# A hybrid decoder trunk: x load and exchanged rows issued later, two norms by Ln/Exp without reciprocals, and new filler counts

## The reference

```python
h = rms_norm(x, norm_g[l]);  p = h @ w_in[l]
z, p_rw, p_ml, p_mla, p_da = split(p)        # 2048 | 1600 | 2056 | 704 | 1536 columns
y = concat(beta0 * rwkv7(p_rw), beta1 * mlstm(p_ml), beta2 * mla(p_mla), beta3 * diff_attn(p_da)) * silu(z)
x = x + y @ w_out[l]
```

```python
# RWKV-7: the keys that are removed from the state are normalised per head of 64
kk = kk / maximum(sqrt(sum(kk * kk)), 1e-12)
# mLSTM, per head of 128: a normaliser, then an RMS norm over the head
h = num / maximum(abs(den), exp(-m))
h = h * rsqrt(mean(h * h) + eps) * g
```

## Time and profile before

| what | value |
|---|---|
| median of 3 runs (lowest, highest) | 2413.65 us (2412.28, 2413.82) |
| the profiled execution's own time | 2416.05 us |
| its span, first to last instruction | 2414.3 us |
| busy: PE, weight loads, DVE, ACT, POOL | 2324.0, 1751.9, 1192.2, 634.9, 1737.8 us |
| mean granted clock of PE | 0.990 |
| moved by DMA | 285.09 MB, mean 118 GB/s |

### The profile page before, as it was taken

One profiled execution on the slowest core, in us unless ns is written; L12 is line 12 of the kernel. 1 busy time (PEld: TensorE's weight loads), 2 busy tenths in 40 slices (PEclk: granted clock), 3 DMA queues, 4 the chain that ended last, 5 costly groups with the idle time before them and its releaser, 6 DMA issues. The chain is left out here.

```text
span 2414.3 us, 38594 instructions
## 1 busy us (share of the span) xinstructions
PE 2324.0 (96%) x16160; PEld 1751.9 (73%) x16160; DVE 1192.2 (49%) x1515; ACT 634.9 (26%) x1133; POOL 1737.8 (72%) x1228
## 2 busy tenths in 40 slices
PE   7999999999999999899999999999999999989999
PEld 6767777777777777677777677777776777767777
DVE  5123346647464773565250323557375546735552
ACT  5222222212221222333341323222222212214421
POOL 3677688768577787687637666878586687877785
PEclk9999999999999999999999999999999999999999
DMA  4623253223234346432445233533242243473323
GB/s 156 187 80 104 83 161 110 84 81 114 84 89 132 118 131 233 151 92 71 148 112 160 79 114 92 154 93 102 66 121 82 81 150 108 131 275 110 86 77 125
DMA packets 164335, 285.09 MB, mean 118 GB/s; under 512 B 28664, under 2 KB 36216, under 8 KB 162624
## 3 DMA queue, kind: packets, MB, share of 16 engines
q1 hardware_dynamic: 108352, 180.93, 27.0%
q10 hardware_dynamic: 55808, 101.69, 12.4%
HBM read 230.89 MB, written 51.64 MB: 117 GB/s over the span
## 5 line engine op out<-in xcount | busy, mean ns | idle before, releaser
L733 POOL TENSOR_SCALAR w_hi<-raw 128x512 fp32r<-128x512 f32 x552 | 905.4, 1640 | 476.3 <-PE ps_proj L774 401.6
L743 POOL TENSOR_TENSOR w_lo<-raw,w_hi 128x512 fp32r<-128x512 f32 (+1 forms) x640 | 836.8, 1308 | 152.6 <-ACT w_hi L1237 97.1
L774 PE MATMUL ps_proj<-h_hi,w_hi 128*128 128x512 f32 (+1 forms) x1760 | 740.1, 421 | 2.0 <-POOL w_lo L743 0.9
L774 PE MATMUL ps_proj<-h_lo,w_hi 128*128 128x512 f32 (+1 forms) x1760 | 691.8, 393 | 0.0
L774 PE MATMUL ps_proj<-h_hi,w_lo 128*128 128x512 f32 x1728 | 678.5, 393 | 0.0
L774 PEld LDWEIGHTS ps_proj<-h_hi,w_hi 128*128 128x128 f32 (+1 forms) x1760 | 331.3, 188 | 113.1 <-issue 29.7
L774 PEld LDWEIGHTS ps_proj<-h_lo,w_hi 128*128 128x128 f32 (+1 forms) x1760 | 331.3, 188 | 75.0
L774 PEld LDWEIGHTS ps_proj<-h_hi,w_lo 128*128 128x128 f32 x1728 | 327.8, 190 | 68.6 <-issue 11.4
L789 PE MATMUL ps_proj<-w_hi,h_hi 128*128 128x512 f32 x448 | 181.1, 404 | 0.4 <-POOL w_lo L743 0.4
L789 PE MATMUL ps_proj<-w_hi,h_lo 128*128 128x512 f32 x448 | 174.9, 390 | 0.0
L789 PE MATMUL ps_proj<-w_lo,h_hi 128*128 128x512 f32 x448 | 174.5, 390 | 0.0
(11 more groups left out here) (349 smaller groups left out, 3132.5 us busy)
## 6 DMA issues: line engine op xcount, KB each, us to landing
raw<-in_w_in_dram SPq DMA_DIRECT2D x480, 256.0 KB, 2.7
raw<-in_w_out_dram SPq DMA_DIRECT2D x128, 256.0 KB, 3.0
projected<-stage ACTq DMA_DIRECT2D x116, 256.0 KB, 2.8
arena<-projected ACTq DMA_DIRECT2D x90, 256.0 KB, 3.1
out_dram<-arena ACTq DMA_DIRECT2D x7, 1024.0 KB, 4.8
gated_hi<-arena ACTq DMA_DIRECT2D x24, 256.0 KB, 2.6
gated_lo<-arena ACTq DMA_DIRECT2D x24, 256.0 KB, 3.2
h_hi<-gated_hi SPq DMA_DIRECT2D x8, 768.0 KB, 13.7
```

Of the source, the lines that this page charges most:

```text
L733: nc.gpsimd.tensor_scalar(hi, src, 1.0, None, ALU.mult).then_inc(s_hi_split, 1)
L743: nc.gpsimd.tensor_tensor(lo, src, hi.bitcast(F32), ALU.subtract).then_inc(s_raw_split, 1)
L774: last = mm(ps_proj[rows, m, :], lhsT, rhs, start=(k == 0 and j == 0), stop=(k == KT - 1 and j == len(products) - 1))
```

## The change

On ACT, the load of x moves from ahead of DA's head 0 to behind head 0's exponentials, and the exchanged rows of the next head move from between the two halves to behind both. kk's norm becomes exp(-0.5 Ln(sum)) on ACT, ahead of the decay's exponentials, and one DVE operation. mLSTM's norm is computed without dividing: PE does the denominator first, ACT squares the numerator, DVE forms eps * d^2 and adds it to the mean, ACT takes Ln and Exp. A tiny Ln (load_ln) is put ahead of three waits, so that ACT's table is loaded there. FILL has new counts.

```diff
-    rw_first=8, rw_lora=(10, 10, 10, 9), rw_factors=(31, 33, 33, 33), ...
+    rw_first=8, rw_lora=(10, 11, 11, 11), rw_factors=(26, 28, 28, 28), ...
-    rw_carried=(2, 2, 2, 2), rw_mean=(3, 3, 3, 3), rw_gate=(13, 14, 13, 12),
-    ml_first=25, ml_qk=(19, 10, 10, 10), ml_s=(8, 7, 7, 6), ml_h=(14, 14, 13, 11), ml_gate=(7, 12, 12, 12),
-    da_first=21, ..., da_half=(12, 17, 15, 16), ...
+    rw_carried=(2, 2, 2, 2), rw_mean=(4, 4, 4, 4), rw_gate=(13, 14, 13, 12),
+    ml_first=25, ml_qk=(19, 13, 13, 13), ml_s=(8, 8, 8, 8), ml_h=(3, 3, 3, 3), ml_gate=(15, 15, 15, 12),
+    da_first=21, ..., da_half=(14, 17, 15, 16), ...
@@ PE, mLSTM
                         for i in range(NT):
-                            mm(ps[:, 0, i * P:T], ml_v[:, i, h * P:(h + 1) * P], ml_s[:, i, i * P:T], ...)
-                        for i in range(NT):
                             last = mm(ps[:, 1, i * P:T], ones, ml_s[:, i, i * P:T], ...)
+                        last.then_inc(s_ml_den_mm, 1)
+                        for i in range(NT):
+                            last = mm(ps[:, 0, i * P:T], ml_v[:, i, h * P:(h + 1) * P], ml_s[:, i, i * P:T], ...)
                         last.then_inc(s_ml_num_mm, 1)
@@ ACT
+                    def load_ln():
+                        link(nc.scalar.activation(table_set, eps_col, ACT.Ln))
@@ ACT, RWKV
                         fill("rw_lora", hp)
+                        load_ln()
+                        act.wait_ge(s_rw_kk_sum, hp + 1)
+                        link(nc.scalar.activation(rw_nr, ps[:, 3, :], ACT.Ln))
+                        nc.scalar.activation(rw_nr, rw_nr, ACT.Exp, scale=-0.5).then_inc(s_rw_kk_root, 1)
                         act.wait_ge(s_rw_decay, hp + 1)
...
                         nc.scalar.activation(rw_wi, rw_c, ACT.Exp, scale=-1.0).then_inc(s_rw_decay_exp, 1)
-                        act.wait_ge(s_rw_kk_sum, hp + 1)
-                        nc.scalar.activation(rw_nr, ps[:, 3, :], ACT.Sqrt).then_inc(s_rw_kk_root, 1)
                         fill("rw_factors", hp)
...
                         fill("rw_mean", hp)
+                        load_ln()
                         act.wait_ge(s_rw_var, hp + 1)
@@ ACT, mLSTM
+                        act.wait_ge(s_ml_num_mm, h + 1)
+                        nc.scalar.activation(ml_sq, ps[:, 0, :], ACT.Square).then_inc(s_ml_h_sq, 1)
                         fill("ml_h", h)
-                        act.wait_ge(s_ml_h_sum, h + 1)
-                        rstd(ml_rs, ps[:, 2, :], P, EPS).then_inc(s_ml_h_rs, 1)
+                        load_ln()
+                        act.wait_ge(s_ml_h_var, h + 1)
+                        link(nc.scalar.activation(ml_rs, ml_den, ACT.Ln))
+                        nc.scalar.activation(ml_rs, ml_rs, ACT.Exp, scale=-0.5).then_inc(s_ml_h_rs, 1)
                         fill("ml_gate", h)
@@ ACT, DA
                     act.dma_start(da_const, ...)
-                    act.dma_start(x_tok, x_dram if tail else a["x"][0]...).then_inc(s_x_prefetched, 16)
                     fill("to_z_da")
...
                             act.wait_ge(s_da_row_max, 2 * h + half + 1)
-                            if half and h < HEADS - 1:
-                                load_da_swapped(h + 1)
                             for b in range(4):
                                 ...   # the exponentials
+                        if h < HEADS - 1:
+                            load_da_swapped(h + 1)
                         if h == 0:
+                            act.dma_start(x_tok, x_dram if tail else a["x"][0]...).then_inc(s_x_prefetched, 16)
                             fill("da_half", h)
@@ DVE, RWKV
-                        link(v.tensor_scalar(rw_nr, rw_nr, 1e-12, None, MAX))
-                        link(v.reciprocal(rw_nr, rw_nr))
-                        link(v.tensor_tensor(rw_kk, rw_kk, rw_nr, MUL))
+                        link(v.scalar_tensor_tensor(out=rw_kk, in0=rw_nr, scalar=1e12, in1=rw_kk, op0=MIN, op1=MUL))
@@ DVE, mLSTM
-                        dve.wait_ge(s_ml_num_mm, h + 1)
+                        dve.wait_ge(s_ml_den_mm, h + 1)
                         link(v.scalar_tensor_tensor(out=ml_den, in0=ps[:, 1, :], scalar=-1.0, in1=ml_nf, op0=MUL, op1=MAX))
-                        link(v.tensor_tensor(ml_den, ps[:, 1, :], ml_den, MAX))
-                        link(v.reciprocal(ml_den, ml_den))
-                        link(v.tensor_tensor(ml_h, ps[:, 0, :], ml_den, MUL))
-                        v.tensor_tensor(ml_sq, ml_h, ml_h, MUL).then_inc(s_ml_h_sq, 1)
+                        link(v.scalar_tensor_tensor(out=ml_den, in0=ps[:, 1, :], scalar=DEN_MIN, in1=ml_den, op0=MAX, op1=MAX))
+                        link(v.scalar_tensor_tensor(out=ml_den, in0=ml_den, scalar=EPS, in1=ml_den, op0=MUL, op1=MUL))
+                        dve.wait_ge(s_ml_h_sum, h + 1)
+                        v.scalar_tensor_tensor(out=ml_den, in0=ps[:, 2, :], scalar=1.0 / P, in1=ml_den, op0=MUL, op1=ADD).then_inc(s_ml_h_var, 1)
                         dve.wait_ge(s_ml_o_tanh, h + 1)
                         dve.wait_ge(s_ml_h_rs, h + 1)
-                        link(v.scalar_tensor_tensor(out=ml_h, in0=ml_h, ..., in1=ml_rs, op0=MUL, op1=MUL))
+                        link(v.scalar_tensor_tensor(out=ml_h, in0=ps[:, 0, :], ..., in1=ml_rs, op0=MUL, op1=MUL))
```

More of the change, by code:

```diff
@@ L39 @@
 MASKED = -1e30
+DEN_MIN = 1e-15
 Z0 = 0
@@ L98 @@
     la_probs=(13, 13, 13, 13), la_turned=(3, 3, 3, 3), la_gate=(4, 4, 4, 4),
-    rw_first=8, rw_lora=(10, 10, 10, 9), rw_factors=(31, 33, 33, 33), rw_turned=(3, 3, 3, 3), rw_v=(2, 2, 2, 2),
+    rw_first=8, rw_lora=(10, 11, 11, 11), rw_factors=(26, 28, 28, 28), rw_turned=(3, 3, 3, 3), rw_v=(2, 2, 2, 2),
     rw_gram=(4, 4, 4, 4), rw_x=(2, 2, 2, 2), rw_level=(1, 1, 1, 1), rw_step=(1, 1, 1, 1), rw_levels=(1, 1, 1, 1),
     rw_pu=(2, 2, 2, 2), rw_local=(4, 4, 4, 4), rw_outer=(1, 1, 1, 1), rw_state=(1, 1, 1, 1), rw_state_last=(0, 0, 0, 0),
-    rw_carried=(2, 2, 2, 2), rw_mean=(3, 3, 3, 3), rw_gate=(13, 14, 13, 12),
-    ml_first=25, ml_qk=(19, 10, 10, 10), ml_s=(8, 7, 7, 6), ml_h=(14, 14, 13, 11), ml_gate=(7, 12, 12, 12),
-    da_first=21, da_sums=(14, 10, 10, 10), da_scores=(6, 6, 6, 6), da_half=(12, 17, 15, 16), da_turned=(3, 3, 3, 3),
+    rw_carried=(2, 2, 2, 2), rw_mean=(4, 4, 4, 4), rw_gate=(13, 14, 13, 12),
+    ml_first=25, ml_qk=(19, 13, 13, 13), ml_s=(8, 8, 8, 8), ml_h=(3, 3, 3, 3), ml_gate=(15, 15, 15, 12),
+    da_first=21, da_sums=(14, 10, 10, 10), da_scores=(6, 6, 6, 6), da_half=(14, 17, 15, 16), da_turned=(3, 3, 3, 3),
     da_osq=(3, 4, 3, 3), da_gate=(9, 10, 10, 10))
@@ L403, in build @@
         lam_prod = small[:, 29:31]
-        sqrt_set = small[:, 60:61]
+        table_set = small[:, 60:61]
         neg_f32 = carve(D, P)
@@ L638, in build @@
         s_ml_num_mm = sem("ml_num_mm")
+        s_ml_den_mm = sem("ml_den_mm")
+        s_ml_h_var = sem("ml_h_var")
         s_ml_h_sq = sem("ml_h_sq")
@@ L1145, in _ @@
                         for i in range(NT):
-                            mm(ps[:, 0, i * P:T], ml_v[:, i, h * P:(h + 1) * P], ml_s[:, i, i * P:T],
-                               start=(i == 0), stop=(i == NT - 1))
+                            last = mm(ps[:, 1, i * P:T], ones, ml_s[:, i, i * P:T],
+                                      start=(i == 0), stop=(i == NT - 1))
+                        last.then_inc(s_ml_den_mm, 1)
                         for i in range(NT):
-                            last = mm(ps[:, 1, i * P:T], ones, ml_s[:, i, i * P:T],
+                            last = mm(ps[:, 0, i * P:T], ml_v[:, i, h * P:(h + 1) * P], ml_s[:, i, i * P:T],
                                       start=(i == 0), stop=(i == NT - 1))
@@ L1308, in _ @@
                         act.wait_ge(s_setup, 32)
-                        link(nc.scalar.activation(sqrt_set, eps_col, ACT.Sqrt))
+                        link(nc.scalar.activation(table_set, eps_col, ACT.Sqrt))
                     if tail:
@@ L1594, in _ @@
                     act.dma_start(da_const, a["const"][:, DA_CONST[0]:DA_CONST[1]]).then_inc(s_da_first_loaded, 16)
-                    act.dma_start(x_tok, x_dram if tail else a["x"][0].rearrange("(i p) d -> p i d", p=P)
-                                  ).then_inc(s_x_prefetched, 16)
                     fill("to_z_da")
@@ L1619, in _ @@
                                 nc.scalar.activation(da_p[:, b, 0:(i + 1) * P], ps[:, b, 0:(i + 1) * P], ACT.Exp, scale=da_rq[:, 4 * half + b:4 * half + b + 1], bias=da_mx[:, b:b + 1], accum_out=da_sum[:, b:b + 1]).then_inc(s_da_probs_exp, 1)
+                        if h < HEADS - 1:
+                            load_da_swapped(h + 1)
                         if h == 0:
+                            act.dma_start(x_tok, x_dram if tail else a["x"][0].rearrange("(i p) d -> p i d", p=P)
+                                          ).then_inc(s_x_prefetched, 16)
                             fill("da_half", h)
```

2 lines of the change are left out of this document (1 added, 1 removed).

## The result

The changed kernel takes 2373.9 us (median of 4 runs, 2372.4 to 2377.5), the kernel before beside it 2413.74: 39.8 us less (ratio on record 0.9828 [0.9816, 0.9841]; the two medians divide to 0.9835). The forecast was 2373.5 us. The profiled execution took 2377.48 us (span 2375.7), 38.6 less than that of before, against 40.1 in the sum. It is the slowest of the four; its mean granted clock is 0.996, that of the others 0.998. The total is right to 0.4 us; several of its terms are not, and their errors cancel.

What follows compares the result with a forecast made beforehand. The prediction took TensorE as the bound: its fixed work, 90 us standing still and lower-clock losses. Gains of 55.7 us less losses of 15.6 gave net 40.1, hence 2373.5 us by the median, range 2357 to 2389.

Steps and rivals of the forecast that it cites:

- The x load: First DA scores, head 0, both layers: moving x removes the wait, 21.6 us, and the low clock behind it, 4.9 us.
- The argument about the pair: DA head 0: exchanged rows pass SP's y pair, since engines alternate between queues, so no wait; the opposing rival had 15%.
- The exponentials 1.34 us earlier: DA transposes: without the four row issues ahead, exponentials come 1.34 us earlier for heads 0 to 2; 7.2 us together.
- mLSTM head 1: Gate with 15 tiles covers the chain, so PE's 2.9 us waits go: 6.2 us, plus 6.9 us of clock.
- scores and numerators: mLSTM head 2: waits of 1.1 and 1.2 us go with 3 and 1 more tiles, 3.0 us.
- RWKV's mean: One extra tile at the mean removes four PE waits of 0.5 us, 2.8 us.
- RWKV's pair 3: Wait for the squares, 1.4 us in both layers, goes with 2 more tiles, 3.1 us.
- (a): Group 191's end in ml_first: ACT's copies come late behind the stored-y wait and loads; 8.0 us, plus 3.4 of clock.
- (b): Group 207's end in ml_qk of mLSTM head 1: copy behind keep_y and tanh of z, 4.2 us lost, no clock.
- Two are late: Of all group ends under the new fills, only two have ACT bank copies late enough to stop PE.
- load_ln, 0 us: Ln's table load already runs ahead of the wait, so the tiny Ln brings 0 us.
- The weights and GpSimd: Two rivals: weights starve around the x load, 2431 us, 5%; GpSimd becomes the bound, 2378 us, 5%.

Runs made afterwards that it cites:

- x_late: Kernel before with one edit: the load of x stands behind DA head 0's exponentials; 2396.75 us against 2414.45.
- x_late_pair_late: Kernel before with the load of x behind DA head 0's exponentials and SP's y pairs issued three steps later; 2390.13 us against 2413.09.
- tuned: Changed kernel with ends of groups 143, 207 and 223 moved, plus more tiles in DA, scores included, and at the first RWKV pair; 2383.48 us.
- lora13: Changed kernel with ends of groups 143, 207, 223 moved, more tiles at RWKV pair 0 and DA heads 2 and 3, none at scores; 2361.04 us.

## Why the prediction was right, and where not

- **The x load, 21.6 us and 4.9 of the clock.** Right in size (22.9 - 1.6 = 21.3 us at the scores, with the full clock behind them: 8 us from 949 at 1.00). The rows landed in 3.5 us, where up to 10 were allowed. The argument about the pair was thin: what it takes from the rule, that the rows pass the pair, did not come out in x_late. That no wait came is true only because the new fills put the pair behind the rows, which the prediction did not work out, and in so far it is luck; x_late without them gives 17.7 us, x_late_pair_late 23.0.
- **The exponentials 1.34 us earlier, 7.2 us.** Mis-sized: the transposes' wait for DVE fell by 6.3 us, but PE now waits 1.6 us for ACT's copy (L1227) at head 0, so 4.7. By itself it gave 3.4. Head 1 gained as foreseen. Head 2 waits 1.3 us as before, because the same six DVE operations behind the exponentials took 5.4 us (1056.49 to 1061.90) where they took 4.0 before the change (1080.30 to 1084.28). That used up the 1.34. What the slow ones among them ran beside is in the last section.
- **mLSTM head 1, 6.2 and 6.9 us of the clock; scores and numerators 3.0; RWKV's mean 2.8.** All gone as foreseen, and RWKV's pair 3 (3.1 us) too: of 5.0 us in three waits one of 2.1 is left, which the prediction did not speak of.
- **(a), 8.0 and 3.4 us.** The place and the order are right, the size is not: 0.65 us for the first tile where 3.3 were forecast, 2.0 with all four where 4.4 were, 4.1 in both layers for 8.0, and no low clock. (The 0.4 "there today" is not: at 753 to 757 in the trace of before no product starts late.) The step that failed took the end of ACT's loads from the trace of before (764.96). There ACT waits until y of pair 3 has landed, 4.64 us after its issue, with four stores of group 191 just ahead of it in the queue. With the new fills those stores come behind, y lands in 2.25 us, and the four loads begin at 748.19. So counted from PE's sum of squares (746.18 before, 734.07 now) the loads end at 16.5 us instead of 18.8. Moving a group's end behind a wait seems to take its stores out of the way of that wait too; no run moved the stores alone.
- **(b), 4.2 us.** The first tile waits 1.18 us instead of 1.8; with all four 2.5 us are lost, as forecast, and 5.1 in both layers, since there is no 0.4 of "today" to take off here either.
- **"Two are late".** Wrong, four are. Group 143 ends in the second tile of `rw_lora` of pair 2, with half of its copies behind the stores of y and ACT's tanh: 0.89 us in layer 0, 1.65 in layer 1 with 1.7 us of clock. Group 223 ends in `ml_gate` of head 2 (before: `ml_s`), with the copy behind the head's Ln and Exp: 0.3 us in each layer. I looked at the ends of groups around mLSTM head 1 and not at the others. The late copies cost PE 23.8 - 8.2 = 15.6 us more than before, against 12.2 forecast for two places.
- **load_ln, 0 us.** Right: 2373.3 without it. That "the trace differs" is too much said: here too the load is ACT's last instruction before the activation, and only the activation waits.
- **The Ln and Exp in place of the reciprocal.** Right that nothing is gained by DVE's 60 us as such.
- **The weights and GpSimd.** Neither rival shows: PE's first scores and the tiles around x do not wait for w_lo, and POOL's busy time is 8.8 us less.

The balance, by the measured terms: gains 21.3 + 4.9 + 4.7 + 6.2 + 6.9 + 3.0 + 3.1 + 2.8 = 52.9. Losses are 15.6 of late copies, 1.7 of clock behind group 143 and 1.7 of clock at 1146, which nothing foretold (last section), 19.0 in all. Net 33.9, where 55.7 - 15.6 = 40.1 were forecast and 38.6 measured. So the gains were put 2.8 us too high. Among the losses (a) with its clock was put 7.3 us too high, and two places and their clock were left out. 4.7 us of the measured gain are in none of these terms; small waits that went make up 1 to 2 of them, the rest stays open. That the total comes out to 0.4 us is luck.

How the 39.8 us divide, by runs: x 17.7, rows 3.4, norms 2.5, and the new fills 16.7 on top, together 40.3. Each of these differences is uncertain by 2 to 4 us, and some 5 of the 16.7 are not fillers' gain in mLSTM or RWKV but the pair and the rows moved apart (17.7 against 23.0).

## What to carry to other kernels

When filler work moves, list every place at which a group or a column ends, and read at each what stands ahead of the copy or the addition in that engine's order, and the wait ahead of it as well: such places cost as much (15.6 us here, 19.4 in tuned) as a whole part of the change brings. A large load belongs behind every small transfer of its queue that someone waits for, stores too, and the other queue has to be looked at for the same moment. An arithmetic change that shortens work which filler work covers already brings nothing until the filler work is dealt out anew.

## What was not expected of the hardware

- The four transfers of exchanged rows (32 KB each) landed 17.3, 8.9, 6.9 and 3.5 us after their last issue, by what ran beside them, and a store issued 9 us behind a 4096 KB load on its queue let ACT go on only after 14 us.
- The same DVE operation has two durations. L2027 on 128x512 took 0.98 us at 1056.57 in tuned and, in the changed kernel's head 2:

```profile
1059.51 0.71 DVE L2026 TENSOR_SCALAR arena<-arena 128x512 f32<-128x512 f32 x1
1060.26 1.64 DVE L2027 SCALAR_TENSOR_TENSOR arena<-arena 128x512 f32<-128x512 f32 x1
```

  The traces show what goes with it. Beside the slow one GpSimd runs the second operation of its split:

```profile
1060.03 1.32 POOL L748 TENSOR_TENSOR w_lo<-raw,w_hi 128x512 fp32r<-128x512 f32 x1
```

  In the changed kernel 41 DVE operations of this kind (SCALAR_TENSOR_TENSOR, 128x512, nothing from PSUM) begin while L748 runs, and all 41 end 0.54 to 0.56 us behind its end, whatever its rest; their median is 1.66 us. The 53 that begin beside GpSimd's other operation (L738) have a median of 0.98, the 20 with GpSimd idle 0.69. The kernel before shows the same (41, with 0.54 to 0.56 us). The four waits of 1.3 us that are left at the transposes are at heads 2 and 3 in both layers, where L2027 takes 1.64 us; at head 1 it takes 0.98 and PE waits for nothing. lora13 has one more tile at heads 2 and 3: at head 3 L2027 then takes 0.98 us and the wait is gone, at head 2 it takes 1.64 and the 1.3 us stay. So what 1.34 us on ACT are worth depends on where GpSimd's next operation falls. No run moved GpSimd's work alone; that it is the cause is argued from this pattern.
- The Trainium skill (ScalarE: Activation LUTs, section Table sets: the hidden batching unit) lists a set that holds both Ln and Exp. Here each Exp behind an Ln has a load of its own, 1.28 us, as in the changed kernel's RWKV norm:

```profile
735.18 0.60 ACT L1281 ACTIVATE arena<-ps 128x512 f32<-128x512 f32 x1 [15.55 <-PE ps L1118]
735.80 1.28 ACT L1282 ACT_TABLE_LOAD   x1
```

  These loads stand in every Ln/Exp chain, before and after, and change nothing in the comparison. The new norm for kk and mLSTM would be 1.28 us shorter without one.
- The length of the last wait does not settle what the clock does. Behind the same wait of 2.21 us (at the barrier of all engines, L2046; it ends at 1146.19 in the changed kernel and at 1168.63 in the kernel before) it fell in the changed kernel (first row) and not in the kernel before (second row):

```profile
1145.00:1150.00 5.00, 3.81 (x10) 3.11 (x11) 3.53 (x10) 1.49 (x2) 3.65 (x3) 0.66 0.11 30
1170.00:1175.00 5.00, 5.00 (x24) 4.14 (x23) 2.40 (x6) 1.28 (x3) 4.83 (x5) 1.00 0.19 52
```

  It was 0.67 in 1945 to 1950, with no wait over 0.3 us in the ten before; it fell behind a wait of 1.65 us (1735) and not behind one of 1.5 us in the kernel before. Each such stretch costs 1.7 us; the 0.002 of granted clock by which the profiled execution is below the others are 4.8 us of its span.
